# A paired expert layer on Trainium2: coefficients kept in three contiguous pieces, keys chosen in another order, first activations fetched at another point

## The reference, cut to what matters

```python
def block(xb):                                   # 128 tokens
    q = (xb @ w_q).reshape(128, 8, 2, 128)       # 8 heads, two half queries
    s = einsum('thpd,hpkd->thpk', q, subkeys)    # 128 scores per half
    s1, i1 = top_k(s[:, :, 0], 16)
    s2, i2 = top_k(s[:, :, 1], 16)
    cand = s1[..., :, None] + s2[..., None, :]   # 256 candidates per head
    top, pos = top_k(cand, 16)
    idx = expert numbers (i1 * 128 + i2) at pos
    g = softmax(top)
    act = gelu(einsum('td,thkd->thk', xb, u[idx]))
    return einsum('thk,thkd->td', g * act, v[idx])
```

## Time and profile before

| what | value |
|---|---|
| median of three runs (lowest to highest) | 4701.01 us (4680.74 to 4704.79) |
| profiled execution | 4686.01 us |
| its span | 4684.2 us |
| TensorE busy | 4087.9 us (87%) |
| VectorE busy | 3273.8 us (70%) |
| ACT busy | 2026.7 us (43%) |
| POOL busy | 1150.1 us (25%) |
| granted TensorE clock, mean | 0.938 |

### The profile page before, as it was taken

The page is one execution under the profiler, slowest core; times in us unless marked ns, Lnnn a source line. Parts: engine busy times, 40 slices in busy tenths (PEclk is TensorE's granted clock), DMA queues, the critical chain, the costliest instruction groups (busy, mean ns, idle before and its releaser), DMA issues. The chain is left out here.

```text
span 4684.2 us, 74402 instructions
## 1 busy us (share of the span) xinstructions
PE 4087.9 (87%) x28286; PEld 3883.9 (83%) x28286; DVE 3273.8 (70%) x5799; ACT 2026.7 (43%) x3493; POOL 1150.1 (25%) x1007
## 2 busy tenths in 40 slices
PE   6777988879899997848999999699898989989798
PEld 4655887879899996738999999599787989978798
DVE  5865699668688886466987688566575676657566
ACT  4142333657533333324544444344463444446344
POOL 0000000657688883010049545100000000000000
PEclk8888998999999998978999999899898999989899
DMA  6403354998899994405876788455324545532453
GB/s 223 146 32 126 100 163 133 300 288 289 280 328 334 332 333 171 168 9 184 253 244 218 236 298 300 154 182 167 113 78 142 184 154 180 168 107 84 140 185 126
DMA packets 304585, 896.19 MB, mean 191 GB/s; under 512 B 62128, under 2 KB 97936, under 8 KB 303334
## 3 DMA queue, kind: packets, MB, share of 16 engines
q1 hardware_dynamic: 215094, 673.80, 42.7%
q0 software_dynamic: 55520, 201.60, 12.8%
q10 hardware_dynamic: 33616, 16.02, 1.3%
HBM read 834.92 MB, written 56.14 MB: 190 GB/s over the span
## 5 line engine op out<-in xcount | busy, mean ns | idle before, releaser
L153 DVE TENSOR_TENSOR weight_lo<-weight_ring,weight_hi 128x1024 fp32r<-128x1024 f32 x1084 | 1354.5, 1250 | 873.1 <-ACT weight_hi L148 856.4
L148 ACT ACTIVATE weight_hi<-weight_ring 128x1024 fp32r<-128x1024 f32 x1084 | 1141.7, 1054 | 1330.4 <-issue 683.6
L185 PE MATMUL pair0e_acc<-pair_xh,weight_hi 128*128 128x384 f32 (+1 forms) x1152 | 411.8, 357 | 21.5 <-ACT pair0e_gelu L2336 18.9
L185 PE MATMUL pair0e_acc<-pair_xl,weight_hi 128*128 128x384 f32 (+1 forms) x1152 | 400.2, 347 | 0.0
L185 PE MATMUL pair0e_acc<-pair_xh,weight_lo 128*128 128x384 f32 (+1 forms) x1152 | 399.6, 347 | 0.0
L185 PE MATMUL pair0e_acc<-pair0e_coef_hi,weight_hi 128*128 128x384 f32 x1024 | 343.2, 335 | 16.3 <-DVE pair0e_coef_lo L2067 16.3
L185 PE MATMUL pair0e_acc<-pair0e_coef_lo,weight_hi 128*128 128x384 f32 x1024 | 342.8, 335 | 0.0
L185 PE MATMUL pair0e_acc<-pair0e_coef_hi,weight_lo 128*128 128x384 f32 x1024 | 342.8, 335 | 0.0
L185 PE MATMUL peer10e_dot<-peer_xh,weight_hi 128*128 128x224 f32 (+1 forms) x1152 | 324.9, 282 | 8.3 <-DVE weight_lo L153 5.9
L185 PE MATMUL peer10e_dot<-peer_xl,weight_hi 128*128 128x224 f32 (+1 forms) x1152 | 318.0, 276 | 0.0
L185 PE MATMUL peer10e_dot<-peer_xh,weight_lo 128*128 128x224 f32 (+1 forms) x1152 | 318.0, 276 | 0.0
(11 more groups left out here) (617 smaller groups left out, 12376.2 us busy)
## 6 DMA issues: line engine op xcount, KB each, us to landing
weight_ring<-in_w_tiles SPq DMA_DIRECT2D x572, 512.0 KB
weight_ring<-in_peer_tiles SPq DMA_DIRECT2D x512, 512.0 KB
pair_acts<-pair0e_gelu SPq DMA_DIRECT2D x64, 384.0 KB
pair0e_act_in<-pair_acts SPq DMA_DIRECT2D x64, 384.0 KB
peer_acts<-peer10e_gelu SPq DMA_DIRECT2D x64, 224.0 KB
peer10e_act_in<-peer_acts SPq DMA_DIRECT2D x64, 224.0 KB
pair_coefs<-pair0e_G ACTq DMA_DIRECT2D x8, 1536.0 KB
pair0e_kept_in<-pair_coefs SPq DMA_DIRECT2D x64, 192.0 KB
```

Of the source, the lines that this page charges most:

```text
L148: act.activation(self.tile_of(self.hi, g), self.ring[:, g % RING, :], ACT.Copy).then_inc(self.hi_done, 2)
L153: dve.tensor_tensor(self.tile_of(self.lo, g), self.ring[:, g % RING, :], self.tile_of(self.hi, g).bitcast(F32), ALU.subtract).then_inc(sel ...
L185: last = pe.matmul(out, lhsT, rhs, start=start and i == 0, stop=stop and i == len(passes) - 1, **more)
```

## The change

It has these parts:

* G is laid out as three pieces of 64 tokens, each contiguous per partition ([P, 3, 128, 64] in place of [P, 128, 192]). The DRAM copy of the latent coefficients has the same order, so that a drain DMA moves 8 KB in one run per partition where it moved runs of 384 B (96 tokens). The latent stream is drained in three pieces of four DMAs in place of two halves of four. `kept_in`, and POOL's two multiplications, follow the new order.
* The calls of `choose` for all four token tiles come first, score tile pair by score tile pair; then `top_k` for the four token tiles. VectorE takes 3 pieces per step in steps 8 to 32 (before: 1), and 2 or 3 in turn after that (before: 3). By the program, the routing of the four token tiles ends at steps 83, 100, 116 and 131 (before: 52, 79, 105 and 132), and spreading begins a step earlier.
* In both expert layers the first `fetch` is issued at tile 140 of 144 of the first half, after `store(60)`.
* `token_rows`, the copy of the sparse tokens' turned rows, moves from the start of ACT's program to step 8.
* Two guards on PAIR_POOL_HOTS, which stays 1.

```diff
@@ peer_experts, sync
+                if n == front - 4:
+                    for k in range(ACTS_IN - 1):
+                        fetch(k)
             for k in (NKEYS // 2 - 2, NKEYS // 2 - 1):
                 store(k)
-            for k in range(ACTS_IN - 1):
-                fetch(k)
@@ pair_experts
+PIECES = 3
+PIECE = PAIR_OWN // PIECES
-        G = S.sb("G", [P, NKEYS, OWN])
+        G = S.sb("G", [P, PIECES, NKEYS, PIECE])
-        kept_in = S.sb("kept_in", [P, ACTS_IN, 2, OWN])
+        kept_in = S.sb("kept_in", [P, ACTS_IN, PIECES, 2, PIECE])
-        drained = [S.sem("drained%d" % i) for i in range(2)]
+        drained = [S.sem("drained%d" % i) for i in range(PIECES)]
+        piece_groups = own_groups // PIECES
@@ vector
             def routing(step):
+                for c in range(0, QT, 2):
+                    for b in range(4):
+                        yield from choose(b, c)
                 for b, (s, tt) in enumerate(BOTH):
-                    for c in range(0, QT, 2):
-                        yield from choose(b, c)
                     yield from top_k(b, step)
...
-                for _ in range(0 if m < 8 else 1 if m <= 2 * QT else 3):
+                for _ in range(0 if m < 8 else 3 if m <= 2 * QT else 2 + m % 2):
@@ sync
-                sync.dma_start(kept_in[:, slot, :, :],
-                               coefs_dram[2 * k * P:(2 * k + 2) * P, :].rearrange("(a p) t -> p a t", p=P)
+                sync.dma_start(kept_in[:, slot, :, :, :].rearrange("p g a t -> p g (a t)"),
+                               coefs_dram[:, 2 * k * PIECE:(2 * k + 2) * PIECE].rearrange("(g p) c -> p g c", p=P)
                                ).then_inc(act_arrived[slot], 16)
...
+                if n == front - 4:
+                    for piece in range(PIECES):
+                        sync.wait_ge(drained[piece], 16 * 4)
+                    for k in range(ACTS_IN - 1):
+                        fetch(k)
             for k in (NKEYS // 2 - 2, NKEYS // 2 - 1):
                 store(k)
-            for half in range(2):
-                sync.wait_ge(drained[half], 16 * 4)
-            for k in range(ACTS_IN - 1):
-                fetch(k)
@@ gpsimd
-                pool.tensor_tensor(weight[:, j % 2, 0:OWN], act_in[:, slot, j % 2, 0:OWN], kept_in[:, slot, j % 2, :], ALU.mult)
-                pool.tensor_tensor(weight[:, j % 2, OWN:DN], act_in[:, slot, j % 2, OWN:DN], G[:, j, :],
-                                   ALU.mult).then_inc(weighed, 1)
+                out, act = (b.rearrange("p (s g t) -> p s g t", s=2, g=PIECES)
+                            for b in (weight[:, j % 2, :], act_in[:, slot, j % 2, :]))
+                pool.tensor_tensor(out[:, 0], act[:, 0], kept_in[:, slot, :, j % 2, :], ALU.mult)
+                pool.tensor_tensor(out[:, 1], act[:, 1], G[:, :, j, :], ALU.mult).then_inc(weighed, 1)
@@ scalar
-            act.wait_ge(x_turned, 1)
-            act.wait_ge(kept, 16)
-            (the copy of xt, at the start)
+            def token_rows(): (the same, called at m == 8)
-            def drain(half):
-                act.wait_ge(spread_out, (half + 1) * own_groups // 2)
-                some = slice(half * OWN // 2, (half + 1) * OWN // 2)
+            def drain(piece):
+                act.wait_ge(spread_out, (piece + 1) * piece_groups)
                 for i in range(4):
-                    js = slice(i * NKEYS // 4, (i + 1) * NKEYS // 4)
-                    act.dma_start(coefs_dram[i * NKEYS // 4 * P:(i + 1) * NKEYS // 4 * P, some].rearrange("(j p) t -> p j t", p=P),
-                                  G[:, js, some]).then_inc(drained[half], 16)
+                    some = slice(i * NKEYS // 4, (i + 1) * NKEYS // 4)
+                    act.dma_start(coefs_dram[piece * P:(piece + 1) * P, some.start * PIECE:some.stop * PIECE],
+                                  G[:, piece, some, :].rearrange("p j t -> p (j t)")).then_inc(drained[piece], 16)
...
-                    if s == 1 and own % (own_groups // 2) == 0:
-                        act.wait_ge(drained[own // (own_groups // 2)], 16 * 4)
-                    act.activation(G[:, :, own * GROUP:(own + 1) * GROUP],
+                    piece, at_piece = divmod(own, piece_groups)
+                    if s == 1 and at_piece == 0:
+                        act.wait_ge(drained[piece], 16 * 4)
+                    act.activation(G[:, piece, :, at_piece * GROUP:(at_piece + 1) * GROUP],
@@ build
-    dram["pair_coefs"] = nc.dram_tensor("pair_coefs", (NKEYS * P, PAIR_OWN), F32).ap()
+    dram["pair_coefs"] = nc.dram_tensor("pair_coefs", (PIECES * P, NKEYS * PIECE), F32).ap()
```

More of the change, by code:

```diff
@@ L2181, in _ @@
                 if m < 2 * front:
-                    for g in spread_steps.get(m + PAIR_LEAD, ()):
-                        one_hots(g)
+                    if PAIR_POOL_HOTS:
+                        for g in spread_steps.get(m + PAIR_LEAD, ()):
+                            one_hots(g)
                     continue
@@ L2222, in spread @@
                     pe.wait_ge(scores_out, QT)
-                pe.wait_ge(first_done, g + 1)
+                if PAIR_POOL_HOTS:
+                    pe.wait_ge(first_done, g + 1)
                 pe.wait_ge(second_done, g + 1)
@@ L2277, in _, with token_rows @@
         def _(act):
-            act.wait_ge(x_turned, 1)
-            act.wait_ge(kept, 16)
-            for half in range(2):
-                cols = slice(half * 512, half * 512 + 512)
-                last = act.activation(xt[:, cols], flat[:, D + half * 512:D + half * 512 + 512], ACT.Copy)
-            last.then_inc(xt_done, 1)
+            def token_rows():
+                act.wait_ge(x_turned, 1)
+                act.wait_ge(kept, 16)
+                for half in range(2):
+                    cols = slice(half * 512, half * 512 + 512)
+                    last = act.activation(xt[:, cols], flat[:, D + half * 512:D + half * 512 + 512], ACT.Copy)
+                last.then_inc(xt_done, 1)
             def soften(b):
@@ L2322, in _ @@
                 W.next_hi(act, 2 * q0 + m)
+                if m == 8:
+                    token_rows()
                 gelu_rows(m)
@@ L2351, in _ @@
                     act.wait_ge(multiplied, g + 1)
-                    if s == 1 and own % (own_groups // 2) == 0:
-                        act.wait_ge(drained[own // (own_groups // 2)], 16 * 4)
-                    act.activation(G[:, :, own * GROUP:(own + 1) * GROUP],
+                    piece, at_piece = divmod(own, piece_groups)
+                    if s == 1 and at_piece == 0:
+                        act.wait_ge(drained[piece], 16 * 4)
+                    act.activation(G[:, piece, :, at_piece * GROUP:(at_piece + 1) * GROUP],
                                    product[:, g % 2, :].rearrange("p (t j) -> p j t", t=GROUP),
                                    ACT.Copy).then_inc(spread_out, 1)
-                    if s == 0 and own % (own_groups // 2) == own_groups // 2 - 1:
-                        drain(own // (own_groups // 2))
+                    if s == 0 and at_piece == piece_groups - 1:
+                        drain(piece)
                 for g in spread_steps.get(m + PAIR_LEAD, ()):
```

## The result

The changed kernel takes 4636.31 us (median of 4 runs, 4622.25 to 4641.29) where the kernel before, timed beside it, took 4697.84 (4680.74 to 4704.79): ratio 0.9874, 95% interval 0.9854 to 0.9895. That is 61.5 us less; 4620 was forecast. Timed again later, beside other variants, it took 4636.34 us (0.9869, 0.9849 to 0.9889). The profiled execution took 4622.25 us, span 4620.5; it is the lowest of the four.

What follows compares the result with a forecast made beforehand. Bounds by stretch: TensorE for queries and second half, VectorE in routing; spreading lost time to ACT's drain holes. Gains 39.5 + 19 + 12 = 70.5 from 4686 gave 4615.5, taken as 4620 for a median; range 4590 to 4662.

Steps and rivals of the forecast that it cites:

- Drains, holes gone: Spreading stretch: contiguous drain pieces stop ACT's long holds, so TensorE's two holes vanish; 47.5 us gained.
- rival 3: Spreading stretch: ACT is still held, by bytes, so the drain gain is lost; 4660 us as a median; chance 0.05.
- ACT's issues were to be under 1 us each: Sign for the drains, with no 10 us lacking matmuls between 880 and 1150; wrong if ACT sits again.
- Drains, contention: Spreading stretch: drain bursts press on the row gathers; 8 us lost, from 0 to 36.
- the weight ring holds four tiles and coefficients run two tiles ahead, so most is absorbed: Spreading stretch: reason for taking the drains' contention loss as 8 us, between 0 and 36.
- rival 1: Spreading stretch: drain bursts cost their whole DMA time, 36 us in place of 8; 4648 us; chance 0.15.
- the rule of the Trainium skill: DMA engines go round queues packet by packet: a drain gets about a third, 19 us late for three pieces; 4631.
- The sign that I named for it: Contention would show as VectorE's wait for rows in spreading, 58 us before, up by more than 30.
- Choosing order: Routing stretch: choosing keys as scores come hides VectorE work in the earlier stage; 19 us gained, from 0 to 26.
- rival 2: Routing: choosing earlier gains nothing, as VectorE's early load or the wait at each turn offsets it; 4639; chance 0.11.
- Early fetch: Gap between halves: first activations fetched early save 6.5 us in the paired layer, 5.6 in the single; together 12.
- The slower rival: Second half: dearer weighing makes POOL the bound; 4816 us if weighing doubles; chance 0.03.

Runs made afterwards that it cites:

- E4: Changed kernel with the twelve drain DMAs issued early, in steps 10 to 26, from another tile, so no drain traffic beside the gathers; 4612.97 us (0.9824).
- order alone: Kernel before with only the new order of routing and its numbers of pieces per step; 4665.58 us (0.9941).
- E8: Kernel before, old layout, with its eight drain DMAs issued one by one, five groups apart, in place of two bursts of four; 4655.87 us (0.9932).
- the layout alone: Kernel before with only the new layout in three pieces and its drains; 4668.59 us (0.9955).
- E6: Changed kernel, bursts kept, each 8 KB of a drain written as four runs of 2 KB with 64-byte gaps in DRAM; 4631.61 us (0.9878).
- E12: E11 with four routing pieces per step in place of three in steps 8 to 32, then 2 1/4 in place of 2 1/2; 4622.81 us (0.9846).
- E5: Changed kernel with its twelve drain DMAs issued one by one, four groups apart, in place of three bursts of four; 4633.0 us (0.9879).
- E11: Changed kernel with drain runs of 2 KB and its twelve drain DMAs issued one by one, four groups apart; 4627.35 us (0.9856).
- E10: Kernel before with the new order and early fetch, old layout, eight drain DMAs issued five groups apart, `token_rows` at its old place; 4623.66 us (0.9848).
- E9: The changed kernel measured again, unaltered, for its spread and a second profile; 4636.34 us (0.9869).

## Why the prediction held, and which term was off

*Drains, holes gone (47.5 predicted):* the size holds, 50.9 by E4, or 46.6 against order alone. The reason was half right. The hold is no price per descriptor, as E8 shows, but comes of what stands in the queue before a DMA; "so many microseconds per DMA" (6.0, in rival 3) was an average over one free issue and several waits. ACT's issues were to be under 1 us each; the median is 0.55, the longest 1.8, so four in a row still wait a little.

*Drains, contention (8 predicted):* this is the mis-sized term. It measures 21.8 us by E4, so spreading gained 29.1 in place of 39.5 (25.8 by the layout alone). The step that failed is "the weight ring holds four tiles and coefficients run two tiles ahead, so most is absorbed". Weights are covered by the ring; the gathered rows are not, and VectorE's program puts the one-hots that TensorE needs next behind the wait for a row. Of the 21.8 us, 12.8 are TensorE's waits before `spread`; the one that was followed through the timeline is of this kind. I had priced the wait of the gathers and not what is queued behind it. The measured 21.8 lies between my 8 and the 36 of rival 1, next to the 19 that the rule of the Trainium skill gave there. The size is near, the split that I drew from the rule is not: I took equal turns for equal bytes, a third each, and the drain had 40 to 60% of the DMA time in its first 12 us, 2.63 of 4.96 MB in the first. The nearness is in part luck. The sign that I named for it was badly put as well: VectorE's wait for rows rose from 58.2 to 81.6 us from the window of the earlier trace rows to 785:1215 here (66.8 to 81.6 over the whole stretch), less than the 30 that I wanted for contention, while the loss was there. E6 has a wait of 57.0 and a spreading stretch only 3.4 us shorter, so that wait doesn't measure the cost.

*Choosing order (19 predicted):* 20.6 us. VectorE's extra work in the first stage is hidden (42.9 of 64 us busy, TensorE 324 records as before), and TensorE is full in 527 to 600 us. E12 shows room for 10.9 more in the routing, of which the time shows 4.5; rival 2 is out.

*Early fetch (6.5 + 5.6 predicted):* 6.7 + 5.5. The gap is 9.6 us against the "near 10" forecast.

*Moving `token_rows` (nothing predicted):* the last `score` matmul starts at 536.0 us in the changed kernel and at 534.9 before, so nothing was gained ahead of the routing. No run has this edit alone.

*POOL with three runs of 64:* weighing takes 1.01 and 1.20 us against 1.02 and 1.17 in the earlier trace rows, second half of the changed kernel (count, busy us, mean ns):

```profile
L2174 POOL TENSOR_TENSOR pair0e_weight<-pair0e_act_in,pair0e_G 128x192 f32<-128x192 f32 x126 | 151.6, 1203 | 0.0
L2173 POOL TENSOR_TENSOR pair0e_weight<-pair0e_act_in,pair0e_kept_in 128x192 f32<-128x192 f32 x126 | 127.4, 1011 | 67.4 <-DMA pair0e_kept_in<-pair_coefs 35.2 <-DVE pair0e_coef_lo L2072 30.8
```

Half 2 is 1.5 us longer, and 536.0 to 542.2 over all variants, with either layout. The slower rival is out, and so is rival 3.

*The sum:* 29.1 + 20.6 + 6.7 + 5.5 = 61.9 in place of 70.5, and the spans differ by 63.7. The profiled execution came out 7 us above the 4615.5 of the sum. The rest of the 16 us between 4620 and 4636 is the allowance from one execution to a median: I added 5, and the profiled execution of the changed kernel is 14 below its median.

*Open:* 21.8 us of contention are there by E4, 23.4 with the gap, and none of E5, E6 and E11 gets back more than 8.7 of these 23.4. That would point to the bytes themselves, which only a stage with free DMA could take; that wasn't tried in a form that keeps the reference's coefficients. But E8 speaks against it: it moves the same bytes in the same stretch, and its spreading takes 417.8 us, only 6.6 more than E4, with 7.4 us of waits of TensorE before `spread`. E10, with the same drains and the new order, takes 425.7. Whether E8's profile was a lucky one (it is 11 us below the median of its runs) or the old order suits the drains better is not known. Why E10 gains 12.7 us by the median over E9 where the table shows 5.5 in spreading plus gap is not settled either.

## What to carry to other kernels

When an engine stands behind its own DMA issues, look at the single issues before blaming their descriptors: if the first is short and the next ones long (0.39 and 9.65 us here), try moving them apart; here that removed the wait with no change of layout. When a burst displaces other transfers, follow the late transfer through the in-order program of whoever waits for it: here the price was what stood behind that wait more than the wait. And when a variant shortens one wait and gains nothing, look for the wait that grew in its place, as in E6. Work of a bound engine that only needs early inputs belongs in the stage in which that engine idles.

## What was not expected of the hardware

- One DMA of 4,096 runs of 384 bytes is issued from ACT in 0.37 us, as one of 128 runs of 8 KB is (0.33). Four of the first in a row took 22.0 and 26.1 us, four of the second 2.3 to 4.2, and four with 512 runs of 2 KB 3.6 to 9.3.
- The share of DMA time that the drain queue took beside two busy queues, in the first 12 us of the first burst, was 53, 48 and 58% with packets of 8, 2 and 0.4 KB; over all bursts it was 40 to 60, 48 to 63 and 46 to 58%.
- 12.58 MB of drain in three bursts cost spreading 21.8 us at a DMA share of 0.89. Issued one by one over 160 to 184 us they cost 19.0 (E5), 14.0 (E11) and 14.5 (E10), each against E4; E8, with the old order, is only 6.6 above E4.
